# Two transformer-like blocks on one core: the second block's input norm from narrow sums, its product opened two tiles at a time

## The reference, cut to what matters

```python
def first_block(x, ...):
    ...
    h = rms_norm(x, norm_ffn_pre[l])
    f = (jax.nn.silu(h @ w_ffn_gate[l]) * (h @ w_ffn_up[l])) @ w_ffn_down[l]
    x = x + rms_norm(f, norm_ffn_post[l])
    return x

def second_block(x, norm1_g, w_in, ...):
    ...
    h = rms_norm_2(x, norm1_g[l])
    z = h @ w_in[l]
    a, gate, q, k, v = jnp.split(z, splits, axis=-1)
    ...

def rms_norm_2(x, g):
    xf = x.astype(jnp.float32)
    y = xf * lax.rsqrt(jnp.mean(xf * xf, axis=-1, keepdims=True) + EPS)
    return (y * g.astype(jnp.float32)).astype(x.dtype)
```

## Time and profile before

| | us |
|---|---|
| median of three runs | 1456.49 (1456.46 to 1457.65) |
| the profiled execution's own time | 1456.94 |
| its span | 1455.2 |
| TensorE busy | 1444.2 (99%) |
| VectorE, ScalarE, GpSimd busy | 677.4, 585.4, 653.8 |

### The profile page before, as it was taken

How to read it: one execution, slowest core, us unless ns; L and a number is a source line. 1 busy time by engine, 2 the same in 40 slices (tenths; PEclk the granted TensorE clock), 3 DMA queues, 4 the chain that set the end, 5 groups by cost and what they waited for, 6 DMA issues and landing times.

```text
span 1455.2 us, 19531 instructions
## 1 busy us (share of the span) xinstructions
PE 1444.2 (99%) x7020; PEld 1171.3 (80%) x7020; DVE 677.4 (47%) x1093; ACT 585.4 (40%) x922; POOL 653.8 (45%) x304
## 2 busy tenths in 40 slices
PE   9999999999999999999999999999999999999999
PEld 6888888788788778888888887777678888888887
DVE  6426656775525285333331018989664333333000
ACT  5243435665643253332232225666654223222221
POOL 4434324762244434444444452766134444444443
PEclk9999999999999999999999999999999999999999
DMA  5422211111133223233233333322122223323333
GB/s 188 148 88 87 87 58 58 45 59 59 46 100 101 96 78 96 93 101 99 89 101 101 114 103 131 102 65 66 45 76 99 96 92 101 100 88 101 105 111 118
DMA packets 38573, 134.15 MB, mean 92 GB/s; under 512 B 4496, under 2 KB 4752, under 8 KB 38512
## 3 DMA queue, kind: packets, MB, share of 16 engines
q1 hardware_dynamic: 37248, 130.70, 27.5%
q10 hardware_dynamic: 1264, 2.62, 0.6%
HBM read 131.20 MB, written 2.10 MB: 92 GB/s over the span
## 4 chain that ended last, share of the span: by engine, by line
PE 74%; issue 14%; DVE 5%; POOL 4%; ACT 1%; DMA 0%; POOLq 0%; SPq 0%; DVEq 0%
PE bank L1177 18%; PE bank L1178 18%; PE bank L1179 18%; POOL wL L497 4%; PE bank L1530 3%; PE bank L1532 2%; PE bank L1531 2%; PE bank L1206 1%; PE bank L1208 1%; PE bank L1207 1%; PE bank L1309 1%; PE bank L1307 1%; PE bank L1308 1%; DVE bank L2291 1%; PE bank L1585 1%
## 5 line engine op out<-in xcount | busy, mean ns | idle before, releaser
L497 POOL TENSOR_TENSOR wL<-raw,wH 128x1024 fp32r<-128x1024 f32 x234 | 574.1, 2453 | 745.6 <-ACT wH L593 620.5
L593 ACT ACTIVATE wH<-raw 128x1024 fp32r<-128x1024 f32 x209 | 221.3, 1059 | 586.5 <-PE bank L1179 520.4
L1177 PE MATMUL bank<-aH,wH 128*128 128x512 f32 x920 | 359.5, 391 | 0.4 <-POOL wL L497 0.4
L1179 PE MATMUL bank<-aH,wL 128*128 128x512 f32 x920 | 358.0, 389 | 0.0
L1178 PE MATMUL bank<-aL,wH 128*128 128x512 f32 x920 | 358.0, 389 | 0.0
L1177 PEld LDWEIGHTS bank<-aH,wH 128*128 128x128 f32 x920 | 172.7, 188 | 38.7 <-issue 1.0
L1178 PEld LDWEIGHTS bank<-aL,wH 128*128 128x128 f32 x920 | 172.7, 188 | 36.2 <-issue 0.5
L1179 PEld LDWEIGHTS bank<-aH,wL 128*128 128x128 f32 x920 | 172.7, 188 | 35.8
L1179 PE MATMUL bank<-fH,wL 128*128 128x512 f32 x352 | 137.0, 389 | 0.0
L1178 PE MATMUL bank<-fL,wH 128*128 128x512 f32 x352 | 137.0, 389 | 0.0
L1177 PE MATMUL bank<-fH,wH 128*128 128x512 f32 x352 | 136.9, 389 | 0.0
(11 more groups left out here) (346 smaller groups left out, 1995.4 us busy)
## 6 DMA issues: line engine op xcount, KB each, us to landing
raw<-in_w SPq DMA_DIRECT2D x234, 512.0 KB, 3.3
bmk<-in_bias SPq DMA_DIRECT2D x6, 512.0 KB, 4.7
out_x<-xT SPq DMA_DIRECT2D x8, 256.0 KB, 3.6
xT<-in_x SPq DMA_DIRECT2D x3, 512.0 KB, 8.2
ct<-in_ct ACTq DMA_DIRECT2D x3, 384.0 KB, 3.7
xT<-in_x SPq DMA_DIRECT2D x2, 256.0 KB, 4.3
raw<-in_w SPq DMA_DIRECT2D x2, 256.0 KB, 4.7
w1k<-in_w1k ACTq DMA_DIRECT2D x1, 512.0 KB, 4.4
```

The costliest lines, as they stand in the source:

```text
L497: pool.tensor_tensor(wL[:, c_slot, :], raw[:, c_slot, :], wH[:, c_slot, :].bitcast(F32), ALU.subtract).then_inc(sem("w_lo"), 1)
L593: act.activation(wH[:, s, :], raw[:, s, :], ACT.Copy).then_inc(sem("w_hi"), 1)
L1177: pe.matmul(bank[:], hi, H[:, ka, :], start=(k == 0), stop=False)
L1179: mm = pe.matmul(bank[:], lo, H[:, ka, :], start=False, stop=(k == p.k - 1))
```

## The change

1. In `dn1` VectorE handles each tile with more work: it accumulates gain² * z² in `squares_of_z` (the storage of `nt_`) and gain * z * x in `products_with_x` (the storage of `nr`). For the last tile it writes z * x to `sq[:, 0]` ahead of the copy. A new small tile holds the squared gains.
2. TensorE sums over channels, four narrow float32 matmuls each: `side_mean` (the mean square of the old residual, kept in `nx`) at block 6 of dn1's last tile, `side_squares` at block 12, `side_products` at block 18, and the last tile's shares of the last two after `k` = 0 and `k` = 1 of the opening. The mean square of the new residual is then mean(x²) + 2 r sum(g z x)/D + r² sum(g² z²)/D with the root r of the post norm: five instructions on 128x4 elements of VectorE after the residual's tile 4, Ln and Exp of ScalarE after its tile 5, three more small ones of VectorE, then `spread_root` on TensorE and one copy to `nr` by ScalarE. The eight `add_up`, the squares, and the norm over 128x512 go.
3. The opening takes two tiles at once: for each `k` the four products with `aH`, and from `k` = 2 on the low products of `k` - 2 for both tiles.
4. The low parts `aL` are written by GpSimd from `tmp` (written by ScalarE, a second scaled copy of `xT`) minus `aH`. VectorE's scaled z goes to a PSUM bank (banks 1 and 2 of the next tiles) instead of `tmp`.
5. Chunk c0+2 of the weights goes to a third slot (`third_hi`, `third_lo`, in `mH`), split before the residual's parts; tile 2 uses it.

```diff
@@ SyncE
-                            sp.wait_ge(sem("ffn1_done"), 1)
+                            sp.wait_ge(sem("res2"), KD)
@@ GpSimd
-            pool.wait_ge(sem("ffn1_done"), 1)
+            pool.wait_ge(sem("w_hi"), i2 + 3)
+            pool.tensor_tensor(third_lo, raw[:, i2 % 2, :], third_hi.bitcast(F32), ALU.subtract).then_inc(sem("w_lo"), 1)
+            for kt in range(KD):
+                pool.wait_ge(sem("h3_hi"), kt + 1)
+                pool.wait_ge(sem("h3_x"), kt + 1)
+                pool.tensor_tensor(aL[:, kt, :], tmp[:, kt % 2, :], aH[:, kt, :].bitcast(F32), ALU.subtract)\
+                    .then_inc(sem("h3_lo"), 1)
+            pool.wait_ge(sem("res2"), KD)
...
-                low((i2 + t + 1) % 2, i2 + t + 2)
+                if t > 1:
+                    low((i2 + t + 1) % 2, i2 + t + 2)
@@ ScalarE
-            high_of_x("h3", "g_norm1", "res2", 4, True)
+            act.activation(third_hi, raw[:, p.c0 % 2, :], ACT.Copy).then_inc(sem("w_hi"), 1)
+            for kt in range(KD):
+                act.wait_ge(sem("res2"), kt + 1)
+                act.activation(aH[:, kt, :], xT[:, kt, :], ACT.Copy, scale=vec("g_norm1", kt)).then_inc(sem("h3_hi"), 1)
+                if kt >= 2:
+                    act.wait_ge(sem("h3_lo"), kt - 1)
+                act.activation(tmp[:, kt % 2, :], xT[:, kt, :], ACT.Copy, scale=vec("g_norm1", kt)).then_inc(sem("h3_x"), 1)
+                if kt == 5:
+                    act.wait_ge(sem("side_ready"), 4)
+                    act.activation(side_log, root_x, ACT.Ln).then_inc(sem("ln_ready"), 1)
+                    act.wait_ge(sem("ln_ready"), 5)
+                    act.activation(side_guess, side_log, ACT.Exp, scale=-0.5).then_inc(sem("nr_ready"), 1)
+            act.wait_ge(sem("root_spread"), 3)
+            act.activation(nr[:], B[4][:], ACT.Copy).then_inc(sem("nr_ready"), 1)
...
-            rsqrt(5, B[6][:], D, (sem("sum_ready"), 5), nr[:], B[5][:])
...
-                ahead(p, t - 1)
+                if t > 1:
+                    ahead(p, t - 1)
@@ TensorE
-            gemm(PH["dn1"], fH, fL, first=("ff_fL", 2))
+            def side_sums(out, src, col, start=False):
+
+                for t in range(TT):
+                    mm = pe.matmul(out[:, t:t + 1], src[:, t * P:(t + 1) * P], col, start=start and t == 0, stop=True,
+                                   skip_group_check=True)
+                return mm
+
+            def side_sums_of_tiles(k):
+
+                if k == 6:
+                    side_sums(side_mean, nx, ident[:, 0:1], True)
+                if k == 12:
+                    pe.wait_ge(sem("side_ready"), 1)
+                    side_sums(side_squares, squares_of_z, ones[:, 0:1])
+                if k == 18:
+                    pe.wait_ge(sem("side_ready"), 2)
+                    side_sums(side_products, products_with_x, ones[:, 0:1])
...
+            tile_products(p, 0, 7, 1, fH, fL, after=side_sums_of_tiles)
...
+            for k in range(KD):
                 high_products(k)
+                if k == 0:
+                    side_sums(side_squares, sq[:, 1, :], squared_gains[:, KD - 1:KD])
+                if k == 1:
+                    pe.wait_ge(sem("side_ready"), 3)
+                    side_sums(side_products, sq[:, 0, :], vec("g_ffn_post", KD - 1)).then_inc(sem("sum_ready"), 1)
                 if k >= 2:
+                    pe.wait_ge(sem("h3_lo"), k - 1)
+                    for t in range(2):
+                        low_product(t, k - 2)
+            spread_root(3, B[4])
+            for t in range(2):
+                for k in range(KD - 2, KD):
+                    pe.wait_ge(sem("h3_lo"), k + 1)
+                    mm = low_product(t, k)
+                mm.then_inc(sem("chunk_done"), 1)
@@ VectorE, for each tile t of dn1 after its copy to z2T
+                    squares = dve.scalar_tensor_tensor(squares_of_z[:], sq[:, t % 2, :], squared_gains[:, t:t + 1], squares_of_z[:],
+                                                       ALU.mult, ALU.add)
...
+                to = products_with_x[:] if t == 0 else tmp[:, 0, :]
+                link(dve.scalar_tensor_tensor(to, z2T[:, t, :], vec("g_ffn_post", t), xT[:, t, :], ALU.mult, ALU.mult))
+                if t:
+                    products = dve.tensor_tensor(products_with_x[:], products_with_x[:], tmp[:, 0, :], ALU.add)
@@ VectorE, the residual
-            residual_and_low(z2T, "g_ffn_post", "res2", "h3", "g_norm1", 2, True)
-            dve.wait_ge(sem("res2"), KD)
-            dve.sem_inc(sem("ffn1_done"), 1)
-            norm(5, B[6], B[5])
+            for kt in range(KD):
+                dve.scalar_tensor_tensor(residual_bank(kt)[:], z2T[:, kt, :], vec("g_ffn_post", kt), B[5][:], ALU.mult, ALU.mult)\
+                    .then_inc(sem("res2_mul"), 1)
+                dve.wait_ge(sem("res2_mul"), kt + 1)
+                dve.tensor_tensor(xT[:, kt, :], residual_bank(kt)[:], xT[:, kt, :], ALU.add).then_inc(sem("res2"), 1)
+                if kt == 4:
+                    dve.wait_ge(sem("sum_ready"), 5)
+                    link(dve.tensor_tensor(root_x, side_squares, root, ALU.mult))
+                    link(dve.scalar_tensor_tensor(root_x, side_products, 2.0, root_x, ALU.mult, ALU.add))
+                    link(dve.tensor_tensor(root_x, root_x, root, ALU.mult))
+                    link(dve.scalar_tensor_tensor(root_x, root_x, 1.0 / D, side_mean, ALU.mult, ALU.add))
+                    dve.tensor_scalar(root_x, root_x, EPS, None, ALU.max).then_inc(sem("side_ready"), 1)
```

More of the change, by code:

```diff
@@ L312, in two_blocks_kernel @@
             up = up_[:, :, 0:S + 2 * HP]
+        third_hi, third_lo = (mH[:, 2 * i:2 * i + 2, :].rearrange("p a s -> p (a s)") for i in range(2))
         def slot_of(kind, n):
@@ L336, in narrow, with residual_bank @@
             return bank[:, 0:TT]
+        squares_of_z, products_with_x = nt_, nr
+        side_squares, side_products, side_mean, side_log, side_guess = (B[6][:, TT * i:TT * (i + 1)] for i in range(5))
+        def residual_bank(kt):
+            return B[(PH["in2"].t0 + 2 + kt % 2) % NBANK]
         def cst(name):
@@ L1616, in values, with high_products @@
                 mm.then_inc(sem("na_pv"), 1)
-            bank0, bank1 = (B[(p.t0 + t) % NBANK] for t in range(2))
-            s0, s1 = (p.c0 % 2, (p.c0 + 1) % 2)
-            pe.wait_ge(sem("w_lo"), p.c0 + 1)
-            pe.wait_ge(sem("bank_free"), p.t0 + 1)
-            for k in range(KD):
+            opening = [(B[(p.t0 + t) % NBANK], (p.c0 + t) % 2) for t in range(2)]
+            def high_products(k):
                 b = slice(k * P, (k + 1) * P)
                 pe.wait_ge(sem("h3_hi"), k + 1)
-                pe.matmul(bank0[:], wH[:, s0, b], aH[:, k, :], start=(k == 0), stop=False, skip_group_check=True)
-                pe.matmul(bank0[:], wL[:, s0, b], aH[:, k, :], start=False, stop=False, skip_group_check=True)
-                add_up(k)
@@ L1629, in low_products @@
[L1629 to L1638 removed]
+                for bank, c_slot in opening:
+                    pe.matmul(bank[:], wH[:, c_slot, b], aH[:, k, :], start=(k == 0), stop=False, skip_group_check=True)
+                    pe.matmul(bank[:], wL[:, c_slot, b], aH[:, k, :], start=False, stop=False, skip_group_check=True)
@@ L1640, in _, with low_product @@
+            def low_product(t, k):
+                bank, c_slot = opening[t]
+                return pe.matmul(bank[:], wH[:, c_slot, k * P:(k + 1) * P], aL[:, k, :], start=False, stop=(k == KD - 1),
+                                 skip_group_check=True)
             pe.wait_ge(sem("w_lo"), p.c0 + 2)
             pe.wait_ge(sem("bank_free"), p.t0 + 2)
-            low_products(range(KD - 3))
-            for k in range(2):
+            for k in range(KD):
                 high_products(k)
-            low_products(range(KD - 3, KD)).then_inc(sem("chunk_done"), 1)
@@ L1646, in _ @@
-            for k in range(KD):
-                if k >= 2:
-                    high_products(k)
-                mm = pe.matmul(bank1[:], wH[:, s1, k * P:(k + 1) * P], aL[:, k, :], start=False, stop=(k == KD - 1), skip_group_check=True)
-            mm.then_inc(sem("chunk_done"), 1)
+                if k == 0:
[3 more added lines that the diff above has]
+                    side_sums(side_products, sq[:, 0, :], vec("g_ffn_post", KD - 1)).then_inc(sem("sum_ready"), 1)
@@ new lines, in _ @@
+            for t in range(KD):
+                n, bank = 3 * KD + t, B[(p.t0 + t) % NBANK]
+                dve.wait_ge(sem("sq_ready"), n + 1)
+                if t == KD - 1:
+                    dve.tensor_tensor(sq[:, 0, :], bank[:], xT[:, t, :], ALU.mult).then_inc(sem("side_ready"), 1)
+                dve.tensor_copy(z2T[:, t, :], bank[:]).then_inc(sem("bank_free"), 1)
+                if t == KD - 1:
+                    break
+                if t == 0:
+                    link(dve.tensor_scalar(squares_of_z[:], sq[:, 0, :], squared_gains[:, 0:1], None, ALU.mult))
+                else:
```

(16 more changed lines are left out.)

66 lines of the change are left out of this document (35 added, 31 removed).

## The result

| | kernel before | changed kernel |
|---|---|---|
| median, same chip, 22 runs each | 1455.93 us (1454.01 to 1457.84) | 1458.78 us (1456.26 to 1461.29) |
| the profiled execution's own time, and its span | 1456.94, 1455.2 | 1459.25, 1457.2 |

The ratio is 1.0018, with a 95% interval of 1.0012 to 1.0025. The medians differ by 2.85 us (0.2%), where 1.6 less was forecast, and the time lies above the range given.

A forecast was written before the change was run, and what follows sets the result against it. TensorE was taken to bound the kernel, with VectorE second behind the opening. Terms +2.8 - 4.8 + 0.3 + 0.1 gave -1.6 us, 1454.9 against the median of 1456.49, range 1453.0 to 1457.5.

The forecast's parts named there:

- What bounds the kernel: Whole kernel: TensorE, busy 99% of the span, so time is won only where it gets less or faster work.
- Term A: dn1's last tile: three groups of four narrow matmuls come in on TensorE, +2.8 us (2.7 to 2.8).
- the slower rival with 1464: dn1's tile seams: VectorE pushes GpSimd's split out, TensorE waits 1.3 seven times, +9, 1464; chance 0.07.
- Term B: The opening: products, narrow sums and transposes take TensorE 13.5 us instead of 18.3, -4.8.
- Term C: Waits inside the opening, for VectorE's small instructions and the parts `aH` and `aL`: +0.3 us (0 to 1.5).
- Term D: Behind the opening: later table load and split delay the gated product, eating VectorE's lead; +0.1 us (0 to 0.9).
- VectorE's chain decides: Behind the opening: VectorE, the second bound, sets the time instead of TensorE; 1455.9; chance 0.11.
- The clock: Idle products at the seam: clock not fixed by code; full clock 1454.4, chance 0.12; half clock on products 1456.5, chance 0.10.

The follow-up runs named there:

- experiment 1: Changed kernel, but two of the five small root instructions keep their running value in PSUM; 1457.05 us, ratio 1.0003 to the kernel before.
- experiment 2: On top of experiment 1, the copy of `nr` to `nrc` reads the spread root from PSUM; 1454.69 us, ratio 0.9988 to the kernel before.
- experiment 5: Changed kernel, but ScalarE loads the sigmoid's table before it waits for the spread root and writes `nr`; 1457.29 us, ratio 1.0004 to the kernel before.
- experiment 6: Changed kernel without the three groups of narrow sums in dn1's last tile; 1456.13 us, ratio 1.0 to the kernel before.
- experiment 8: Experiment 2 and experiment 5 together on the changed kernel: PSUM operands plus the earlier table load; 1454.60 us, ratio 0.9990 to the kernel before.
- experiment 7: The changed kernel again, unchanged, beside experiments 5, 6 and 8; 1459.05 us, ratio 1.0019 to the kernel before.
- experiment 3: Changed kernel with two idle full-width float32 products put into tile 5 of in2 on TensorE; 1457.74 us, ratio 1.001 to the kernel before.
- experiment 4: Changed kernel, but ScalarE and GpSimd split tile 6's weight chunk before tile 4's taps; 1457.68 us, ratio 1.0007 to the kernel before.
- experiment 11: Experiment 8 and experiment 4 together: tile 6's chunk also split before the first taps; 1455.86 us, ratio 0.9993 to the kernel before.
- experiment 9: Experiment 8 with dn1's three narrow-sum groups replacing one idle product before and two behind the root's spread; 1457.97 us, ratio 1.0008 to the kernel before.
- experiment 10: Experiment 8 with dn1's three narrow-sum groups replacing two idle products behind the root's spread, the first kept; 1455.34 us, ratio 0.9991 to the kernel before.

## Why the prediction was wrong, point by point

**What bounds the kernel** held. TensorE's own time decides, and each of its two long waits, taken away, came out in the median (experiments 1, 2 and 5).

**Term A** (+2.8) held: 24 narrow passes, 0.90 for the group between products, 2.9 without them in experiment 6. GpSimd's splits in dn1 were not pushed out; the slower rival with 1464 did not come.

**Term B** (-4.8, to 13.5) held once nothing stood in its way: 13.47 and 13.44 in experiments 1 and 8.

**Term C** is where the first error lies. It says of the five small instructions: "One has two SBUF inputs and meets GpSimd". Two met it. The trace at hand showed 0.57 for a meeting, its own upper bound of 1.3 was the true size (1.14 and 1.17), and it came twice: about 2.0 over their 0.16 each, and a wait of 1.67, against +0.3 (0 to 1.5) for all of term C. Under the clock that the forecast assumed at the seam (experiment 7) tile 2 came 21.67 after the seam, where the forecast had 7.09 + 13.8 = 20.9: term C was 1.1 there instead of 0.3.

The second that met it is a `tensor_scalar` with **one** SBUF input that writes SBUF. I had counted it as free after the rule that I cited from the SBUF page of the Trainium skill ("SBUF — State Buffer", section "SBUF: two separate sides"), and I had cited half of it: the same sentence names VectorE operations in a two-port mode as well, and the page "VectorE: DVE Perf Modes" of the Trainium skill, section "Mode 2×_2P — use both read ports for one tensor", has float32 `tensor_scalar` and `tensor_copy` from SBUF to SBUF in that mode and excludes PSUM. Experiments 1 and 2 agree as far as they go: with a PSUM input the `tensor_scalar` takes 0.16 and the copy 0.68 beside the same GpSimd work. That the mode is what shuts them out, no run here shows.

**Term D** (+0.1, 0 to 0.9) is the second. Its parts came as written: the table load after `nr`, the first gated product shut out for 2.48. But it listed as VectorE's next meeting only another gated product, and not the copy of `nr`, the same kind of instruction with one SBUF input; that cost 1.7 more (2.31 instead of 0.62). And it looked for the lateness at head_spread, where VectorE's lead of 0.8 ends. It passed instead from VectorE to ScalarE's sigmoid, table load and taps, to GpSimd's additions, to the split of tile 6's chunk, which had no slack before: 1.84 of wait, where 0.27 had been. From tile 2 to head_spread experiment 7 takes 27.98 + 4.56 = 32.54, against 30.90 before: +1.6, where +0.1 was forecast. I had read the lead of one engine against TensorE and not asked who else waits for that engine. The rival "VectorE's chain decides" had the right engine, at 1455.9, with the wrong place and size.

**The clock.** That the half clock at the seam isn't fixed by the code was right: of the ten profiles with the same code at the seam (the changed kernel and experiments 1 to 8 and 11) only that of experiment 7 has it. That its absence would bring time was wrong for these two kernels. In the changed one `aH` 5 takes it up (experiment 7). In the one before, the last `aH` does, as the timelines of ScalarE and of the weight loads show:

```profile
884.92 0.72 ACT L653 ACTIVATE aH<-xT,pv 128x512 fp32r<-128x512 f32 x1
...
885.70 0.19 PEld L1626 LDWEIGHTS bank<-aH,wH 128*128 128x128 f32 x1 [0.29 <-ACT aH L653]
```

Its `aH` 7 was written at 885.64 and taken as weights at 885.70. The residual pairs, 1.38 apart, had caught up with TensorE's 1.32 for each `k`, so TensorE could not have been through its eight `k` sooner, whatever the clock of the idle passes.

The mean granted clock of the changed kernel is 0.9982 over its 22 runs, 0.9979 in experiment 7, against 0.9988 to 0.9991 of the kernel before in four sets. Within the runs of these two kernels 0.001 of it goes with 0.7 to 1.3 us, so of the loss some 0.5 to 1.0 us goes with it. It falls at 998 us in experiment 7 as in the first profile, 80 us past the change, and between 995 and 1003 in experiments 1, 9 and 10, but not in eight others nor in the kernel before; what brings it there was not tried.
**Outside the span** each run of the changed kernel spends 2.11 us (2.08 to 2.12 in all its variants), the kernel before 1.78. This +0.33 was in no term. Its cause was not tried.

**The sum now.** Seam to head_spread in experiment 7, with term A ahead of it, is 54.21 + 2.8 = 57.0, against 56.29: +0.7, where the forecast had -1.6. Of these 2.3, terms C and D explain 0.8 and 1.5. With 0.33 outside the span and 0.5 to 1.0 with the clock, +0.7 makes 1.5 to 2.0 of the 2.6 (by the ratio) to 2.85 (by the medians). About 1 us stays open. The half clock at the seam in the profile of before is no candidate, as it cost nothing. One is the slow stretch at 998: the two profiled executions of the changed kernel, whose times lie near its medians, both have it, and with their +1.75 behind head_spread in place of the clock's share the sum would be 2.8. Whether it is in most other runs, no profile shows.

## What to carry to other kernels

Before VectorE work is laid beside a busy GpSimd, go through its instructions form by form: not only those with two SBUF inputs, but float32 copies and `tensor_scalar` from SBUF to SBUF, however small; here each waited out most of a GpSimd instruction, and a PSUM operand freed all three. Follow lateness through every engine that waits for the late one, and look for the hand-off that is only just in time, or not quite, in the profile of before. Idle matmuls that keep the clock up are no free slot: put narrow sums in place of them only after a measurement.

## What the runs showed of the hardware that was not expected

- An instruction on 128x4 elements waits out a GpSimd instruction as one on 128x512 does: 1.14 and 1.17 us beside subtractions of 1.30 each; the same two with a PSUM input take 0.16. The copy of 128x512: 2.31 where a split of 2.40 had begun before it, 0.62 where it began before the split, 0.68 from PSUM.
- With the idle full-width products before the opening replaced by narrow sums, the granted clock fell to 0.50 and stayed for 17 us, although TensorE was shown busy for the whole of it. With one group in place of one of the three idle products the stretch was 7 us long (0.50 from 879 to 886).
- A wait of 1.84 us was followed by 3.4 us of half clock in one profile and by full clock in another of the same kernel.
- Half clock under the idle passes at the seam (3.58 us for four instead of 1.88) cost nothing where a later operand was late anyway: tile 2 started 21.67 and 21.68 after the seam.
- The same program reached its seam at 870.50 in one execution and at 871.66 in another, and 0.33 us between the two kernels lies outside the span that the profile shows.
